# Four outputs instead of two at a time in the first slab pair of each weight stage

## What is computed

```python
for layer in range(2):
    g = norm_gains[layer]
    xpn = _rms(hp, g[0])
    if layer % 2 == 0:   # _even_proj: xn @ w_in_even, mixers, then y @ w_out_even
        ...
    else:                # _odd_proj: xn @ w_in_odd, mixer, then y @ w_out_odd
        ...
    hp = hp + _rms(mix_p, g[1])
    hp = hp + _rms(_mlp(_rms(hp, g[2]), w_up[layer], w_down[layer]), g[3])

def _mlp(x, w_up, w_down):
    h = jax.nn.relu(x @ w_up)
    return (h * h) @ w_down
```

## Time and profile before

| | |
|---|---|
| time, median of 3 runs | 2021.03 us (2018.76 to 2028.19) |
| the profiled execution: its own time, its span | 2023.89 us, 2022.2 us |
| PE, busy share of the span | 86% |
| PEld | 76% |
| DVE | 47% |
| ACT | 29% |
| POOL | 4% |
| TensorE clock granted, mean | 0.89 of full |
| moved by DMA | 192.95 MB, 95 GB/s |
| share of PE in the chain that ended last | 80% |

### The profile page before, as it was taken

One profiled execution on the slowest core, in us unless ns is written; L12 is line 12 of the kernel. 1 busy time (PEld: TensorE's weight loads), 2 busy tenths in 40 slices (PEclk: granted clock), 3 DMA queues, 4 the chain that ended last, 5 costly groups with the idle time before them and its releaser, 6 DMA issues.

```text
span 2022.2 us, 30759 instructions
## 1 busy us (share of the span) xinstructions
PE 1734.8 (86%) x11750; PEld 1538.7 (76%) x11750; DVE 942.8 (47%) x1605; ACT 582.1 (29%) x914; POOL 85.0 (4%) x158
## 2 busy tenths in 40 slices
PE   6999575686877899999999899855867999999996
PEld 5999454333333699999999889844546999999996
DVE  4433344435334374444444733386353654444445
ACT  4211111243342352222222531122112532222224
POOL 0000000112222000000000000000000000000000
PEclk9999655687888899999999999977677999999998
DMA  4122300767674212222222222300110222222221
GB/s 166 64 83 83 129 0 0 255 210 251 210 241 140 91 64 84 84 85 87 92 89 85 69 68 94 117 24 0 42 63 31 84 84 84 83 83 83 83 84 46
DMA packets 49188, 192.95 MB, mean 95 GB/s; under 512 B 7197, under 2 KB 9374, under 8 KB 35042
## 3 DMA queue, kind: packets, MB, share of 16 engines
q1 hardware_dynamic: 35938, 139.49, 20.4%
q0 software_dynamic: 13184, 52.55, 7.7%
HBM read 180.34 MB, written 11.68 MB: 95 GB/s over the span
## 4 chain that ended last, share of the span: by engine, by line
PE 80%; DVE 11%; issue 4%; ACT 2%; SPq 1%; DMA 1%; DVEq 0%; POOL 0%; POOLq 0%; ACTq 0%
PE ps L291 20%; PE ps L293 20%; PE ps L292 19%; PE ps L1703 2%; PE ps L1266 1%; PE ps L1238 1%; PE ps L1411 1%; PE ps L1414 1%; PE ps L1877 1%; PE ps L1369 1%; PE ps L1447 1%; PE ps L1872 1%; PE ps L1417 1%; DVE sp L1402 1%; DVE z L1403 1%
## 5 line engine op out<-in xcount | busy, mean ns | idle before, releaser
L291 PE MATMUL ps<-xhi,whi 128*128 128x280 f32 x2112 | 620.8, 294 | 33.1 <-DMA mst<-in_m_in_dram 19.1
L293 PE MATMUL ps<-xhi,wlo 128*128 128x280 f32 x2112 | 619.7, 293 | 0.0
L292 PE MATMUL ps<-xlo,whi 128*128 128x280 f32 x2112 | 618.6, 293 | 0.0
L291 PEld LDWEIGHTS ps<-xhi,whi 128*128 128x128 f32 x2112 | 401.7, 190 | 35.9 <-DMA mst<-in_m_in_dram 19.1
L292 PEld LDWEIGHTS ps<-xlo,whi 128*128 128x128 f32 x2112 | 400.8, 190 | 0.5
L293 PEld LDWEIGHTS ps<-xhi,wlo 128*128 128x128 f32 x2112 | 401.1, 190 | 0.0
L283 ACT ACTIVATE whi<-raw 128x2048 fp32r<-128x2048 f32 x98 | 187.5, 1913 | 538.5 <-PE ps L293 537.6
L287 DVE TENSOR_TENSOR wlo<-raw,whi 128x2048 fp32r<-128x2048 f32 x98 | 224.6, 2292 | 224.7 <-ACT whi L283 224.1
L291 PE MATMUL ps<-dhi,whi 128*128 128x280 f32 x1024 | 299.8, 293 | 5.0 <-DVE wlo L287 4.6
L293 PE MATMUL ps<-dhi,wlo 128*128 128x280 f32 x1024 | 299.4, 292 | 0.0
L292 PE MATMUL ps<-dlo,whi 128*128 128x280 f32 x1024 | 298.6, 292 | 0.0
(11 more groups left out here) (369 smaller groups left out, 1707.8 us busy)
## 6 DMA issues: line engine op xcount, KB each, us to landing
raw<-in_weights_dram SPq DMA_DIRECT2D x98, 1024.0 KB, 4.9
kbuf<-in_k_cache_dram SPq DMA_DIRECT2D x128, 256.0 KB, 3.1
vbuf<-in_v_cache_dram POOLq DMA_DIRECT2D x128, 256.0 KB, 3.4
s0b<-in_gla_in_dram POOLq DMA_DIRECT2D x4, 1024.0 KB, 6.4
out_dram<-s0b POOLq DMA_DIRECT2D x4, 1024.0 KB, 4.1
hT<-in_x_dram SPq DMA_DIRECT2D x2, 1120.0 KB, 8.1
out_dram<-pj POOLq DMA_DIRECT2D x2, 1120.0 KB, 14.9
out_dram<-hT POOLq DMA_DIRECT2D x2, 1120.0 KB, 5.2
```

The costliest lines, as they stand in the source:

```text
L291: pe.matmul(out, whi[:, par, t, :], hi, start=first, stop=False)
L292: pe.matmul(out, whi[:, par, t, :], lo, start=False, stop=False)
L293: return pe.matmul(out, wlo[:, par, t, :], hi, start=False, stop=last)
```

## The change

Only first_pair_pe and three lines in the beside functions change, all of them on PE's list. Within a half, the four outputs of both slabs now go side by side through the blocks k: for each k, four products (12 matmuls). The wait for lo is for both slabs at once. beside(4h + 1) is called after block k = 3, beside(4h + 3) at the end of the half. The wait for p_rs moves from n = 5 to n = 3, since bank 6 is now written from the first block of the second half on. In odd, the wait for the banks is for all four of a half. No instruction is added or removed, and the lists of the other engines are as before.

```diff
             for h in range(2):
-                for par in range(2):
-                    if h == 0:
-                        pe.wait_ge(S["lo"], SLAB0[name] + par + 3)
-                    if wait_bank:
-                        wait_bank(4 * h + 2 * par + 1)
-                    for k in range(KB):
-                        if par == 0:
-                            wait_k(h, k)
-                        for f in range(2):
-                            mm = product(pe, ps[:, 4 * h + 2 * par + f, 0:HALF], par, f * KB + k, xhi[:, k, COLS[h]],
-                                         xlo[:, k, COLS[h]], k == 0, k == KB - 1)
-                            if k == KB - 1:
-                                mm.then_inc(S["done"], 1)
-                    beside(4 * h + 2 * par + 1)
+                if h == 0:
+                    pe.wait_ge(S["lo"], SLAB0[name] + 4)
+                if wait_bank:
+                    wait_bank(4 * h + 3)
+                for k in range(KB):
+                    wait_k(h, k)
+                    for n in range(4):
+                        mm = product(pe, ps[:, 4 * h + n, 0:HALF], n // 2, n % 2 * KB + k, xhi[:, k, COLS[h]],
+                                     xlo[:, k, COLS[h]], k == 0, k == KB - 1)
+                        if k == KB - 1:
+                            mm.then_inc(S["done"], 1)
+                    if k == 3:
+                        beside(4 * h + 1)
+                beside(4 * h + 3)
```

```diff
@@ even_pe
                 if n == 3:
                     pre_sums_pe(pe, "even", 0, 6)
+                    pe.wait_ge(S["p_rs"], 1)
                 if n == 5:
                     pe.wait_ge(S["ev"], 1)
                     pre_sums_pe(pe, "even", 1, 0)
-                    pe.wait_ge(S["p_rs"], 1)
@@ mlp_pe
                     pre_sums_pe(pe, name, 0, 6)
-                if n == 5:
                     pe.wait_ge(S["p_rs"], 2 * NORM[name] + 1)
```

## The result

The changed kernel takes 2072.93 us (median of 4 runs, 2069.32 to 2079.8) against 2019.89 for the kernel before in the same comparison: 53.0 us more, ratio 1.0261 with a 95% interval of 1.0218 to 1.0304. The forecast was 2075 (2060 to 2088), 54.4 us more. The profiled execution has a span of 2078.1 us and took 2079.8.

A forecast was written before the change was run, and what follows sets the result against it. PE bounds the kernel, carrying 80% of the chain that ended last. Later starts, factor waits, later splits and clock losses sum to 54.4 us over six stages: 2078 for the profiled execution, 2075 us median, range 2060 to 2088.

The forecast's parts named there:

- (a): Stage starts, PE waits for both slabs' splits: +6.5 us mlp0 and mlp1, +11.2 odd, +5.8 out0, +0.7 even, 0 out1.
- (b): Between a stage's halves, PE waits for the norm's factor: second half +10.7 us in mlp0, +5.9 odd, +1.4 even.
- (c): Four outputs end together, so next slabs split later: 6.2 us each in out0, out1; 2.3 even; net 0 mlp; 0 odd.
- The clock: PE's clock falls after each new wait: 1.5 us lost per wait, bounds 0 and 2.4, 8 x 1.5 in total.
- the 1.5 us that I had given back: In the mlp down product, the wait before the second slab all but vanishes, and with it 1.5 us of clock.
- The clock that holds: Rival: no clock loss after PE's new waits, so without the 8 x 1.5; sum 42.4 us, time 2063, chance 0.07.
- the one at 2.4 each time: Rival: clock costs 2.4 us after each wait, the MLPs' 1.5 not given back; 64.6 us, time 2086, chance 0.08.
- bunched ends for nothing: Rival: four outputs ending together cost nothing in out0, out1 and even; sum 39.7 us, time 2061, chance 0.05.
- not slower: Rival: at starts of mlp0, mlp1, odd, out0 only input blocks decide, second slab in time; 2021 us, chance 0.02.
- the sum: Stage losses even 4.4, out0 12.0, mlp0 12.2, odd 7.4, out1 6.2, mlp1 12.2: 54.4 us; forecast's chance 0.74.
- the first two rivals: The clock that holds (2063 us, chance 0.07) and the one at 2.4 each time (2086 us, chance 0.08).

The follow-up runs named there:

- e1: Kernel before, matmul order kept, but PE waits for both slabs' splits before a stage's first matmul; 2042.62 us, ratio 1.0121 to the kernel before.
- e8: Changed kernel, but in mlp0, mlp1 and odd the norm's sum comes earlier and ACT makes its factor before eight xhi blocks; 2061.19 us, ratio 1.0209.
- e6: Changed kernel, but in out0 and out1 ACT splits the third slab's high part before emptying outputs 4 and 5; 2073.91 us, ratio 1.0287.
- e3: Kernel before, but each first pair's second half in the new side-by-side order, the factor waited for ahead of it; 2045.83 us, ratio 1.0132.
- e5: Kernel before, but at the end of mlp0 DVE adds three squares before splitting odd's second slab; 2012.36 us, ratio 0.9969.
- e9: Changed kernel run again without any edit, as the measure beside e8; 2069.76 us, ratio 1.0267 to the kernel before.
- e2: Kernel before, but each first pair's first half in the new order, waiting for both slabs, second half in the old order; 2039.38 us, ratio 1.0114.

## Why the prediction was right, point by point

**(a) Both slabs at the start**: forecast waits 6.5, 6.5, 11.2 and 5.8 us at mlp0, mlp1, odd and out0, 0 at out1, 0.7 at even. Measured 6.23, 6.17, 11.79 (of which 0.58 had been there for xlo), 9.77 against 3.95 before, that is 5.82, then 0, and 0.8 in the stage even of e1. The rows that gave them were DVE's, and the earlier trace rows, and e1 shows them alone.

**(b) The factor**: forecast 2.7, 2.8, 2.7 and 1.4 us, measured 2.27, 2.26, 2.26 and 1.11. (The 2.8 comes from no sum in the forecast: its terms give 2.65 in odd as in mlp0.) From the first sum in mlp0 to the start of the second half the forecast had 10.45 us, and it is 775.83 - 765.37 = 10.46. The start of mlp0's second half shifts by 11.0 us against a forecast of 10.7 (from the stage's first possible start, 750.8 to 775.83, against 729.9 to 743.93). That in odd 5 us of the late start would vanish in the old wait for sq also held: odd lost 6.2 us in all with a start 11.2 us late. e8 shows the mechanism.

**(c) Bunched ends**: forecast 4.7 in out0 and out1, measured 4.52 twice. In even PE waited 4.73 instead of 2.59; the forecast had 2.3 more, it is 2.1. The down product of mlp0 began 3.78 us after the second half's end (788.26 to 792.04), forecast 3.7, and its second slab then followed without a wait, as forecast.

**The clock** was the term that was mis-sized, in both directions. After the wait of 6.2 us in mlp0 PE ran 48 matmuls in 765.37 - 757.23 = 8.1 us instead of 6.3, 1.8 lost against 1.5 forecast. After the wait of 2.27 it lost nothing, where I had put 1.5. The stretches in mlp0 from 776 to 788 and from 792 to 796, changed kernel (columns as in the earlier trace rows):

```profile
776.00:788.00 12.00, 12.00 (x94) 12.00 (x95) 5.25 (x11) 4.83 (x10) 0.00 (x0) 1.00 0.00 0
792.00:796.00 4.00, 3.96 (x19) 3.99 (x20) 3.01 (x8) 3.37 (x9) 0.00 (x0) 0.57 0.68 236
```

So mlp0 and odd came out 1.4 and 1.2 us under the forecast. mlp1 came out at 12.5 against 12.2 by luck: behind its wait of 2.26 us nothing was lost where I had put 1.5, and the 1.5 us that I had given back had not been lost there before: around 1639 the kernel before kept its full clock after 2.29 us of waiting, as the stretch shows.

```profile
1636.00:1644.00 8.00, 5.71 (x45) 5.49 (x44) 4.82 (x8) 0.51 (x1) 0.00 (x0) 1.00 0.37 131
```

The rule that I set against (c), the Trainium skill's page Perfetto Trace Analysis, section Matmuls (rotate groups through banks so that evacuation overlaps), is not contradicted by the runs; it speaks of banks, and the wait of 4.52 us was for the split of the next slab, whose buffer comes free by a semaphore counted at the outputs' end (e6).

**The rivals.** The clock that holds would have given 42.4 us in the weight stages, the one at 2.4 each time 64.6, and bunched ends for nothing 39.7; they gave 53.6. e3 refutes the last of them by itself, and e1 refutes not slower. The choice between the sum and the first two rivals is no more than the size of the clock's term, and there the total is near 54.4 partly because misses of 1.5 us went both ways.

## What to carry to other kernels

A loop order that needs more operands before its first instruction moves a wait to the front: look up when the last of the operands is ready in the engine that makes it, and not only how often the consumer waits. Everything that is released by the end of an output (the reuse of a buffer, the factor of a norm) is late by as much as outputs end later, even if the matmuls are the same and run at the same pace. And where an in-order engine waits for another, work behind the waiting instruction that is already possible can be put ahead of it: that was worth 0.3% to the kernel before (e5) and 0.4% to the changed one (e8).

## What the runs showed of the hardware that I had not expected

Whether PE's clock falls after a wait is not settled by the wait's length alone. I counted PE's waits ahead of a product in the weight stages in the eleven profiles (before, changed, e1 to e9), and the products among the next 32 matmuls that started 233 ns apart (the lower level, 1.2 GHz) and not about 129 (2.4 GHz). Behind the 12 waits between 1.0 and 1.3 us there was none; behind the 72 waits of 3.5 us or more there were 11 to 24 each; of the 52 waits between 2.0 and 2.7 us, 27 had 11 or more behind them and 25 had none. The wait of 2.26 us in mlp0 had none in the changed kernel and in e9, and 12 in e6, whose only edit stands in out0 and out1. The twelve microseconds from 766 on, in e9 and then in e6:

```profile
766.00:778.00 12.00, 12.00 (x94) 12.00 (x95) 5.25 (x11) 4.82 (x10) 0.00 (x0) 1.00 0.00 0
```

```profile
766.00:778.00 12.00, 12.00 (x84) 12.00 (x85) 5.20 (x10) 4.45 (x9) 0.00 (x0) 0.88 0.00 0
```

It is no plain toss either: the two profiles of the changed kernel (changed and e9) agree at all six waits of that length, and e1 and e2, which have the same waits, agree at all four. But the wait of 2.6 us in even, up to which before and e5 have the same code, had 11 slow matmuls behind it in one and none in the other. What decides it was not found. A wait of that length costs its own length or some 1.5 us more.

The stretch of the mixers, in which nothing was changed, took 620.0 us before, 623.6 in the changed kernel and 612.8 in e5. It goes with the clock granted there, as the stretch from the end of even to the last slice ahead of out0 shows for the kernel before and for e5:

```profile
54.00:674.00 620.00, 485.43 (x2714) 336.93 (x2714) 248.87 (x558) 155.15 (x247) 72.87 (x135) 0.80 0.43 138
```

```profile
54.00:667.00 613.00, 474.26 (x2714) 327.57 (x2714) 248.80 (x558) 155.01 (x247) 72.87 (x135) 0.83 0.43 139
```

The number of matmuls is the same, 2714; the clock is 0.80 and 0.83. From 60 to 670 us the granted clock is 0.80 in the three of these profiles whose mixers took 620 us or more (before, changed, e3) and 0.83 in e1, e5 and e9 (613). A difference of spans between two profiles of this kernel carries up to 11 us of this, which is why the stages were compared one by one. What sets the clock there was not tried.
